# A padded buffer in a float32 two-layer decoder kernel: all later buffers move by 32 bytes in SBUF

## The chip, the cores and the metric

The kernel runs on one core of a Trainium2 chip. The metric is the device time of one execution in microseconds; lower is better. The kernel before takes 1462.85 us, the median of three runs (1462.66 to 1463.01).

## What is computed

Two decoder layers over 256 tokens of width 1024, in float32. The numerically large parts are plain matrix products; the rest is normalisation and two kinds of attention.

```python
for i in range(DEPTH):                                   # DEPTH = 2
    h = rms_norm(x, attn_norm[i])
    proj = h @ w_in[i]                                   # 1024 x 3072
    sb = rms_norm(stick_breaking_attention(...), sb_out_norm[i])
    df = rms_norm(differential_attention(...), diff_subln[i]) * (1 - lambda_init)
    x = x + concat(sb, df) @ w_out[i]                    # 1024 x 1024
    h2 = rms_norm(x, ffn_norm[i])
    if i % 2 == 0:
        x = x + (silu(h2 @ w_gate) * (h2 @ w_up)) @ w_down          # 1024 x 2816 x 1024
    else:
        x = x + moe_swiglu(h2, ...)                      # top 2 of 8 experts, 1024 x 3584 x 1024
return rms_norm(x, final_norm)
```

## The kernel before

**Weights.** All weights stream from HBM in pieces of 1 MB (128 partitions x 2048 float32). SyncE's queue loads piece n into one of the seven slots of `raw`; slot n % 7 is refilled once VectorE has finished with piece n - 7. TensorE runs these products on float32r data, and the kernel gets float32 accuracy by splitting: ScalarE writes `w_hi`, the rounded part of the piece (`split_hi`, L356), and VectorE writes `w_lo = raw - w_hi` (`split_lo`, L361), each into one of three slots. The activations are split in the same way (`aT_hi`/`aT_lo`, `hT_hi`/`hT_lo`, `xe_hi`/`xe_lo`, `he_hi`/`he_lo`). Each product is then three matmuls: high by high, low by high, high by low.

**Matmuls.** The helper `add` (L511) issues all of them. A matmul has a stationary operand of 128x128, loaded by its own LDWEIGHTS, and a moving operand that is streamed past it. Three callers matter:
- `rows_out` (the v projections, `w_out`, the dense feed-forward) and `expert_block` (the mixture of experts): the activation is stationary and the weights, `w_hi` or `w_lo`, move, 512 columns at a time (256 in the last dense piece).
- `columns_out` (the q and k projections): the weights are stationary and the activation, `aT_hi` or `aT_lo`, moves, 256 columns at a time.
- `scatter` (L927): at the very end, `onehotT` is stationary, and `ye_hi` or `ye_lo` moves, 512 columns at a time; eight matmuls in all, also on float32r data.

A row of the trace writes such a matmul as `ps<-w_hi,xe_hi`; the names do not tell which of the two moves. An expert block is 42 pieces of twelve 512-column matmuls each, interrupted by the transposes of the hidden rows (L950) after every sixth piece. Eight blocks run here.

**Where the buffers lie.** Buffers are allocated in the order of the code, one behind the other along the partition, and the allocator starts each at a multiple of 32 bytes. All offsets of slices that a matmul uses (multiples of 128 or 512 float32) are multiples of 512 bytes, so an operand's place within 64 bytes is that of its buffer. In the program as built, the first byte of the buffers that the text speaks of:

| Buffer | bytes from the partition's start | remainder by 64 |
|---|---|---|
| raw | 16512 | 0 |
| w_hi | 73856 | 0 |
| w_lo | 98432 | 0 |
| xs, hn | 123008, 131200 | 0, 0 |
| gC, the heads' norm weights (L132) | 143616 | 0 |
| cst (constants, among them the identity) | 143904 | 32 |
| aT_hi, aT_lo | 152096, 160288 | 32, 32 |
| xe_hi, xe_lo | 152096, 156192 | 32, 32 |
| hT_hi, hT_lo | 168480, 191008 | 32, 32 |
| ye_hi, ye_lo | 176672, 199200 | 32, 32 |
| yrow, xrow, ab, spl | 184864, 180768, 193056, 199200 | 32 |
| onehotT | 189984 | 32 |
| he_hi, he_lo | 191008, 195104 | 32, 32 |
| sil, hid | 203296, 207392 | 32, 32 |
| att | 211712 | 0 |

The buffer `gC` is written once (L1491, L1493) and read as a per-partition factor (L1024 and L1356 in the second half of each attention).

Of the kernel before, what the change touches and what calls it, by code (L numbers as in the profile page):

```python
# [27 lines left out]
P = 128  # L28
# [4 lines left out]
DEPTH = 2  # L33
# [80 lines left out]
def build(nc, x, w_in, w_out, attn_norm, ffn_norm, sb_out_norm, diff_subln, lambda_q1, lambda_k1,  # L114
          lambda_q2, lambda_k2, rel_bias, dense_w_gate, dense_w_up, dense_w_down, router_w,
          expert_w_gate, expert_w_up, expert_w_down, final_norm, consts, out):
    with ExitStack() as ctx:
        def sb(name, shape, dt=F32, stack=ctx):
            return stack.enter_context(nc.sbuf_tensor(name, shape, dt))
# [9 lines left out]
        hn = sb("hn", [P, TT, D])  # L129
        gain = sb("gain", [P, D])  # L130
        gT = sb("gT", [P, 2 * DEPTH, KT])
        gC = sb("gC", [P, 2, DEPTH])  # L132
        rw = sb("rw", [P, KT, NE])
        cst = sb("cst", [P, CONSTS])
        eps = sb("eps", [P, 1])
# [1707 lines left out]
```

## Time and profile before

| | |
|---|---|
| median of three runs | 1462.85 us |
| the profiled execution | 1462.97 us |
| its span, first to last instruction | 1460.8 us |
| around the span (1462.97 - 1460.8) | 2.2 us |
| TensorE busy | 1434.2 us, 98% of the span |
| VectorE, ScalarE busy | 1127.8 us, 934.4 us |
| 512-column and 256-column matmuls of L511 | 5160 and 864 |

The rows that are quoted further down come from one profiled execution. "PE" is TensorE's matmuls, "PEld" its weight loads, DVE VectorE, ACT ScalarE, POOL GpSimd, SPq SyncE's queue. Matmuls overlap, so the mean duration of one (about 395 ns) is longer than the distance between the starts of two in a row; the distance, called pitch below, is what a stream of matmuls costs.

### The profile page before, as it was taken

The numbers are of one execution on the slowest core, as the hardware profiler recorded it, in microseconds if no ns is written. First come the engines' busy times: TensorE is split into PE (matmuls) and PEld (weight loads), VectorE is DVE, ScalarE is ACT, GpSimd is POOL, SyncE is SP. The second block draws the span as 40 slices with busy tenths as digits, with TensorE's granted clock in tenths as the row PEclk, the third lists the DMA queues.
The fourth block names the chain that finished last, engine by engine and source line by source line (L and its number), as shares of the span: only waits on it lengthen the run. The fifth ranks groups of instructions, "written<-read, shape, count | busy, mean of one in ns | idle before, by whom it ended". The sixth has DMA issues, their size and how long they took to land.

```text
span 1460.8 us, 18431 instructions
## 1 busy us (share of the span) xinstructions
PE 1434.2 (98%) x6979; PEld 1179.6 (81%) x6979; DVE 1127.8 (77%) x852; ACT 934.4 (64%) x753; POOL 32.5 (2%) x51
## 2 busy tenths in 40 slices
PE   7999999999999999999999999999999999999996
PEld 7977888889888788888888888888888888888885
DVE  5664545536856899888888888888888888888896
ACT  4454544435554777777777777777777777767774
POOL 0010000000010020000000000000000000001000
PEclk9999999999999999999999999999999999999999
DMA  9642895555433899999999999999999999999992
GB/s 332 211 144 87 321 361 182 173 191 178 150 116 101 289 369 399 394 378 384 357 376 376 363 381 360 384 356 382 373 355 384 375 361 372 369 385 360 396 386 81
DMA packets 190909, 448.81 MB, mean 307 GB/s; under 512 B 8516, under 2 KB 11403, under 8 KB 190859
## 3 DMA queue, kind: packets, MB, share of 16 engines
q1 hardware_dynamic: 189034, 442.27, 83.4%
q0 software_dynamic: 1616, 5.77, 1.0%
q8 instruction: 34, 0.56, 0.2%
q10 hardware_dynamic: 208, 0.08, 0.0%
q14 instruction: 17, 0.13, 0.0%
HBM read 429.74 MB, written 18.36 MB: 307 GB/s over the span
## 4 chain that ended last, share of the span: by engine, by line
PE 95%; DMA 2%; DVE 2%; ACT 1%; SPq 1%; issue 0%; DVEq 0%
PE ps L511 88%; PE ps L950 2%; DMA raw<-in_w_in 1%; PE ps L634 1%; DMA hn<-bias_scratch 1%; PE ps L658 0%; PE ps L908 0%; PE ps L681 0%; PE ps L592 0%; PE ps L786 0%; DMA bias_scratch<-vrow 0%; DVE w_lo L361 0%; PE ps L623 0%; PE ps L645 0%; PE ps L876 0%; PE ps L646 0%
## 5 line engine op out<-in xcount | busy, mean ns | idle before, releaser
L361 DVE TENSOR_TENSOR w_lo<-raw,w_hi 128x2048 fp32r<-128x2048 f32 x401 | 916.0, 2291 | 233.8 <-ACT w_hi L356 232.2
L356 ACT ACTIVATE w_hi<-raw 128x2048 fp32r<-128x2048 f32 (+1 forms) x401 | 767.6, 1915 | 332.3 <-PE ps L511 327.6
L511 PE MATMUL ps<-w_hi,xe_hi 128*128 128x512 f32 x896 | 249.6, 400 | 0.3 <-DVE xe_lo L1744 0.3
L511 PE MATMUL ps<-w_hi,xe_lo 128*128 128x512 f32 x896 | 245.4, 395 | 0.0
L511 PE MATMUL ps<-w_lo,xe_hi 128*128 128x512 f32 x896 | 244.8, 394 | 0.0
L511 PEld LDWEIGHTS ps<-w_lo,xe_hi 128*128 128x128 f32 x896 | 168.2, 188 | 41.1
L511 PEld LDWEIGHTS ps<-w_hi,xe_lo 128*128 128x128 f32 x896 | 168.2, 188 | 40.5
L511 PEld LDWEIGHTS ps<-w_hi,xe_hi 128*128 128x128 f32 x896 | 164.6, 188 | 36.9 <-issue 0.5
L511 PE MATMUL ps<-w_hi,he_hi 128*128 128x512 f32 x448 | 123.5, 397 | 0.0
L511 PE MATMUL ps<-w_hi,he_lo 128*128 128x512 f32 x448 | 122.7, 395 | 0.0
L511 PE MATMUL ps<-w_lo,he_hi 128*128 128x512 f32 x448 | 122.4, 395 | 0.0
L511 PEld LDWEIGHTS ps<-w_lo,he_hi 128*128 128x128 f32 x448 | 84.1, 188 | 20.6
L511 PEld LDWEIGHTS ps<-w_hi,he_lo 128*128 128x128 f32 x448 | 84.1, 188 | 20.2
L511 PEld LDWEIGHTS ps<-w_hi,he_hi 128*128 128x128 f32 x448 | 83.5, 188 | 19.7
L511 PE MATMUL ps<-w_hi,aT_hi 128*128 128x512 f32 (+1 forms) x320 | 90.9, 393 | 4.6 <-DVE aT_lo L1356 4.0
L511 PE MATMUL ps<-w_hi,aT_lo 128*128 128x512 f32 (+1 forms) x320 | 88.6, 386 | 0.0
L511 PE MATMUL ps<-w_lo,aT_hi 128*128 128x512 f32 (+1 forms) x320 | 88.5, 386 | 0.0
L1024 ACT ACTIVATE he_hi<-ps 128x512 fp32r<-128x512 f32 x56 | 33.6, 600 | 69.5 <-PE ps L950 69.5
L511 PEld LDWEIGHTS ps<-w_hi,aT_hi 128*128 128x128 f32 x320 | 57.9, 188 | 17.4 <-DVE aT_lo L1356 4.5
L511 PEld LDWEIGHTS ps<-w_hi,aT_lo 128*128 128x128 f32 x320 | 60.7, 190 | 13.5
L511 PEld LDWEIGHTS ps<-w_lo,aT_hi 128*128 128x128 f32 x320 | 60.7, 190 | 13.2
L1265 ACT ACTIVATE sil<-ps 128x512 f32<-128x512 f32 x56 | 32.6, 582 | 14.0 <-PE ps L511 14.0
(237 smaller groups left out, 991.5 us busy)
## 6 DMA issues: line engine op xcount, KB each, us to landing
raw<-in_expert_w_gate SPq DMA_DIRECT2D x112, 1024.0 KB, 7.4
raw<-in_expert_w_up SPq DMA_DIRECT2D x112, 1024.0 KB, 7.5
raw<-in_expert_w_down SPq DMA_DIRECT2D x112, 1024.0 KB, 7.2
raw<-in_w_in SPq DMA_DIRECT2D x24, 1024.0 KB, 7.2
raw<-in_dense_w_gate SPq DMA_DIRECT2D x11, 1024.0 KB, 6.4
raw<-in_dense_w_up SPq DMA_DIRECT2D x11, 1024.0 KB, 8.0
raw<-in_dense_w_down SPq DMA_DIRECT2D x11, 1024.0 KB, 4.9
raw<-in_w_out SPq DMA_DIRECT2D x8, 1024.0 KB, 5.1
```

Of the source, the lines that this page charges most:

```text
L356: nc.scalar.activation(w_hi[:, n % SPL, 0:width], raw[:, n % RAW, 0:width], ACT.Copy).then_inc(hi_ready, 1)
L361: nc.vector.tensor_tensor(w_lo[:, n % SPL, :], raw[:, n % RAW, :], w_hi[:, n % SPL, :].bitcast(F32), ALU.subtract).then_inc(lo_ready, 1)
L511: return pe.matmul(o, stationary, moving, start=start, stop=stop, skip_group_check=True)
L634: pe.matmul(bank[:, 0:ZW], neg_tri, spl[:, g % 2, m, :], start=False, stop=False, skip_group_check=True)
L950: last = pe.transpose(ps[:, 7, f * P:f * P + P], hid[:, c % 2, f * P:f * P + P], ident)
L1024: return nc.scalar.activation(dst, src, ACT.Copy, scale=scale)
L1265: nc.scalar.activation(sil[:, c % 2, :], ps[:, c % 2, :], ACT.Silu).then_inc(esilu_done, 1)
```

## The change

`gC` had 4 float32 per partition (16 bytes, in a place of 32). It becomes the first four elements of a buffer `head_gains` of 16 float32 (64 bytes). No instruction is added, removed or moved on any engine, no DMA changes its size or its place in the queue, and every operand keeps its shape and type.

```diff
         gT = sb("gT", [P, 2 * DEPTH, KT])
-        gC = sb("gC", [P, 2, DEPTH])
+        head_gains = sb("head_gains", [P, P // 8])
+        gC = head_gains[:, 0:2 * DEPTH].rearrange("p (a l) -> p a l", a=2)
         rw = sb("rw", [P, KT, NE])
```

All buffers allocated behind `gC` move up by 32 bytes: `aT_hi`, `xe_hi`, `hT_hi`, `he_hi`, `ye_hi`, `onehotT`, `cst` and the others of the table with the remainder 32 now have 0, and `att`, for one, goes from 0 to 32, so that not quite all of them lie at multiples of 64. `raw`, `w_hi`, `w_lo`, `xs` and `hn` stay where they are.

## Rows read from the trace of the kernel before

**Rows 1.** The page: busy time by engine, and the granted clock in 40 slices.

```profile
PE 1434.2 (98%) x6979; PEld 1179.6 (81%) x6979; DVE 1127.8 (77%) x852; ACT 934.4 (64%) x753; POOL 32.5 (2%) x51
...
PEclk9999999999999999999999999999999999999999
```

**Rows 2.** The chain of work that ended last: share of the span by line.

```profile
by line: PE ps L511 88.3%; PE ps L950 1.7%; DMA raw<-in_w_in 0.8%; PE ps L634 0.7%; DMA hn<-bias_scratch 0.6%; PE ps L658 0.5%; PE ps L908 0.4%; PE ps L681 0.4%; PE ps L592 0.3%; PE ps L786 0.3%; DMA bias_scratch<-vrow 0.3%; DVE w_lo L361 0
```

**Rows 3.** The chain in order of time: start us, length us, what, matmuls.

```profile
150.36 30.80 PE ps L511 x132
...
631.58 16.80 PE ps L511 x72
648.81 16.80 PE ps L511 x72
```

**Rows 4.** Groups by shape: busy us, mean ns of one; matmuls, then weight loads.

```profile
L511 PE MATMUL ps<-w_hi,xe_lo 128*128 128x512 f32 x896 | 245.4, 395 | 0.0
...
L511 PE MATMUL ps<-aT_lo,w_hi 128*128 128x256 f32 x256 | 33.0, 281 | 0.0
...
L511 PE MATMUL ps<-w_hi,aT_lo 128*128 128x256 f32 x32 | 9.0, 281 | 0.0
...
L927 PE MATMUL ps<-ye_lo,onehotT 128*128 128x512 f32 x4 | 1.6, 390 | 0.0
...
L511 PEld LDWEIGHTS ps<-w_hi,xe_lo 128*128 128x128 f32 x896 | 168.2, 188 | 40.5
```

**Rows 5.** TensorE in order of time, the kernel's last matmuls: start us, us.

```profile
1444.11 1.10 PE L511 MATMUL ps<-w_hi,he_hi 128*128 128x512 f32 x4
...
1445.97 1.10 PE L511 MATMUL ps<-w_lo,he_hi 128*128 128x512 f32 x4
...
1450.01 0.39 PE L927 MATMUL ps<-ye_hi,onehotT 128*128 128x512 f32 x1
1450.24 0.39 PE L927 MATMUL ps<-ye_lo,onehotT 128*128 128x512 f32 x1
...
1451.15 0.39 PE L927 MATMUL ps<-ye_lo,onehotT 128*128 128x512 f32 x1
```

**Rows 6.** Windows: length, busy us (instructions) PE PEld DVE ACT POOL, clock, DMA share, GB/s.

```profile
1444.00:1447.00 3.00, 3.00 (x14) 2.13 (x12) 0.00 (x0) 0.00 (x0) 0.00 (x0) 1.00 0.00 0
...
520.00:620.00 100.00, 100.00 (x447) 80.86 (x446) 90.75 (x71) 72.84 (x50) 8.73 (x4) 1.00 1.04 392
...
600.00:1000.00 400.00, 400.00 (x1778) 323.30 (x1777) 346.54 (x191) 293.36 (x194) 0.00 (x0) 1.00 1.02 374
```

**Rows 7.** TensorE in order of time, two q and k projections.

```profile
48.56 2.08 PE L511 MATMUL ps<-aT_lo,w_hi 128*128 128x256 f32 x16
50.48 2.08 PE L511 MATMUL ps<-aT_hi,w_lo 128*128 128x256 f32 x16
...
69.16 2.04 PE L511 MATMUL ps<-aT_lo,w_hi 128*128 128x256 f32 x16
71.03 2.04 PE L511 MATMUL ps<-aT_hi,w_lo 128*128 128x256 f32 x16
```

**Rows 8.** Groups by shape, the same work at either remainder, ScalarE and GpSimd.

```profile
L1024 ACT ACTIVATE yrow<-ps 128x1024 f32<-128x1024 f32 x7 | 7.2, 1029 | 6.1 <-PE ps L511 6.1
...
L1156 ACT ACTIVATE hn<-ps 128x1024 f32<-128x1024 f32 x2 | 2.0, 1024 | 1.4 <-PE ps L681 1.4
...
L456 POOL TENSOR_SCALAR_AFFINE_SELECT att<-att 128x256 f32<-128x256 f32 x16 | 6.2, 409 | 32.2 <-ACT att L1105 32.2
L456 POOL TENSOR_SCALAR_AFFINE_SELECT spl<-spl 128x256 f32<-128x256 f32 x16 | 6.2, 408 | 321.1 <-DVE spl L1423 321.1
```

**Rows 9.** Waits, longest in total first: us, times, longest us.

```profile
ACT w_hi L356 <- PE ps L511: 327.6, 287, 8.1
...
ACT w_hi L356 <- DMA raw<-in_w_in: 4.5, 1, 4.5
...
SPq L380 <- DVE w_lo L361: 1139.5, 390, 15.5
```

## The prediction

> **What bounds the kernel now.** Read the page's first two parts first. TensorE is busy for 98% of the span, and the granted clock is at its upper level, 2.4 GHz, in all slices [rows 1]. Then the chain that ended last: 88.3% of it is one line, L511, the split matmuls [rows 2]. Whatever changes the time by more than a few microseconds must change what a matmul of L511 costs. The chain in order of time gives that cost: 72 matmuls in 16.80 us, 132 in 30.80, so 233.3 ns from one start to the next, in the dense and the expert feed-forward alike [rows 3]. That is longer than 512 columns at 2.4 GHz, which are 213.3 ns: each matmul loses 20 ns to something. Three candidates can be dropped by rows. It is not data: ScalarE waits 327.6 us for TensorE's freed slots, SyncE's queue waits 1139.5 us for VectorE to free slots, and ScalarE waits for a landing piece once, 4.5 us [rows 9]. It is not another engine or a DMA in the same memory: between 1444 and 1447 us VectorE, ScalarE, GpSimd and the DMA engines do nothing [rows 6], and the matmuls there start at 1444.11 and, eight later, at 1445.97, which is 1.86 us or 233 ns each, as everywhere [rows 5]. And the clock is 1.00 there. What is left is inside TensorE: the matmul, and the load of the next stationary operand that runs beside it.
>
> **What the change does.** It removes and adds no instruction. It moves `aT`, `hT`, `xe` and `he` from remainder 32 to remainder 0 by 64 bytes, while `w_hi` and `w_lo` stay at 0. Before, in every matmul of L511, one operand starts at remainder 0 and the other at 32: they are 32 apart. After it, both start at 0. This holds for either role, since `columns_out` only swaps which of them moves.
>
> **The other engines: nothing.** The trace has the same work at both remainders. ScalarE copies 1024 elements from PSUM into `yrow` (32) in 1029 ns and into `hn` (0) in 1024 ns, GpSimd masks `att` (0) in 409 ns and `spl` (32) in 408 [rows 8]. At most 5 ns in 1024, with another buffer's data, and both engines wait for TensorE anyway [rows 9]. VectorE's 401 splits touch only buffers that do not move. The buffers that DMAs fill with weights do not move either. I put all of this at 0, and at no more than 1 us either way.
>
> **The 512-column matmuls: the term that decides.** There is one place in the trace where both operands of such a matmul have the same remainder: L927, with `ye_hi` or `ye_lo` moving from 32 and `onehotT` stationary at 32. Its starts are 1450.01, 1450.24 and, five steps after the first of them, 1451.15 [rows 5]: 0.91 us for the last four steps, 227.5 ns each, or 1.14 for five, 228. Rounding of the starts alone makes these good to 2 or 3 ns. The durations say the same more sharply, since they are pitch plus a modelled tail: 390 ns for `ye_lo` against 395 for `xe_lo` [rows 4], 5 ns less on four matmuls of which the first is still settling after the stage's start. And the stage just ahead of it, just as undisturbed, runs at 233 [rows 5, 6]. So two operands with the same remainder appear to cost 6 ns less than two that are 32 bytes apart; I take a new pitch of 227.0, a gain of 6.3 ns. The rows bound it by 5 ns (durations) and 7 ns (starts and rounding) if the mechanism is real, and by 0 if it is not.
>
> The count: 3 x (896 + 448 + 288 + 88) = 5160 matmuls of 512 columns (one of the groups of 896 stands in [rows 4]). 5160 x 6.3 ns = 32.5 us. How much of it is on the path: all L511 matmuls cost 5160 x 0.2333 + 864 x 0.1185 = 1306.2 us, and the chain holds 88.3% of 1460.8 = 1289.9 us of them [rows 2], 98.8%. That leaves 32.1 us.
>
> **The 256-column matmuls.** 864 of them. Here the same addresses give several pitches: sixteen in 1.92 us (48.56 to 50.48), 120 ns each, and sixteen in 1.87 us (69.16 to 71.03), 117 ns [rows 7]. I take their middle, 118.5, for the mean. `columns_out` and the last dense piece, with the roles of the remainders swapped, have the same mean of 281 ns [rows 4], so it does not matter which of the two is at 32. Bounds: all could go to 120, + 864 x 1.5 = + 1.3 us, or gain as much as the wide ones, - 864 x 6.3 = - 5.4 us. I take - 2 us, nearer to the narrow spread that these rows show.
>
> **What comes next when TensorE is faster.** Six pieces and four transposes take 17.23 us now, from 631.58 to 648.81 [rows 3], and 17.23 - 72 x 0.0063 = 16.78 then. Between 600 and 1000 us VectorE is busy for 346.5 of 400 us and ScalarE for 293.4 [rows 6]; the same work in 16.78 / 17.23 = 0.974 of the time makes 89% and 75%. DMA moves 374 GB/s there and would have to move 374 / 0.974 = 384; one stretch of 100 us already shows 392 [rows 6]. The slack in [rows 9] covers it. If that cover were gone, DMA would be late next; the rival below prices that.
>
> **The sum.** 1462.97 - 32.1 - 2.0 = 1428.9 us, so 1429. Against the median of the runs the profiled execution is 0.1 us long, which is nothing here.
>
> **A rule that speaks against it.** The row shows 233.3 ns where 512 columns take 213.3 [rows 3]. The Trainium skill, "TensorE: Matmul & The Clock Gate", section "Step-by-step: what each phase is for", says that TensorE has two independent read ports, so that loading the next weights takes no bandwidth from the running matmul, and gives a warm pitch of about 216 ns. By that rule the two operands' relation in memory is nothing and the change gives 1463. The 233.3 ns in the same clock does not agree with its figure, so something that the rule leaves out is at work. "SBUF — State Buffer", section "Specifications (TRN2)", gives lines of 16 bytes; 32 is a multiple of that, and by lines alone no operand was badly placed before, which again would be 1463.
>
> **The rivals.** *Nothing happens: 1463.* The start of an operand within 64 bytes has no effect, and L927 is quicker for another reason: it loads the same stationary block four times in a row, and it is only eight matmuls long. Or only the moving operand's own start counts (32 in L927, 0 in the wide ones of L511, both before and after): then the wide ones keep 233.3, and only `columns_out` can move, 768 x 1.5 ns = + 1.2 us, 1464. For it: scalar and GpSimd work shows no effect of the remainder at all [rows 8]. Against it: no engine or DMA explains why L511 is slower than L927 in a quiet machine, and the equal means of both 256-column groups speak against a role of the moving operand alone.
>
> *DMA takes the place of TensorE: 1439.* The pitch falls, but the weights can't follow past 380 GB/s. The expert stage moves 374 GB/s [rows 6] for about 970 us (475 to 1447 us), so 374 x 970 / 380 = 955 us in place of 945 at 384: 10 us of the gain are gone. ScalarE would then wait for landings in that stage. Against it: 392 GB/s in [rows 6].
>
> *Slower: 1497.* The loss of 20 ns comes from the moving stream and the weight load meeting at the same place in memory, and starting both on the same 64-byte boundary is the worst case, not the best. The places are then told apart by more than 64 bytes: `xe_hi` after the change is 64 apart from `w_hi` by 128, `onehotT` is 0 apart from `ye_hi`, so L927 need not speak for it. One more loss of the size seen (6.7 ns, 233.3 to 240) in the 5160 matmuls is + 34 us. It decides if the pitch in the first expert block is above 233.3. Against it: L927 is the only sample with another distance, and it is quicker.
>
> **How the numbers follow.** Forecast, faster at 1429: 0.53. DMA-bound, 1439: 0.08. Nothing, 1463 to 1464: 0.28. Slower, 1497: 0.08, and 0.03 for smaller losses of the q and k projections that pass 0.2% (768 x 6.3 ns = 4.8 us). A measurement of this kernel can tell about 0.2% from no change, so 1460 to 1466 is the same. Faster 0.61, same 0.28, slower 0.11. If the mechanism is real the time lies between 1462.97 - 36.1 - 5.4 = 1421.5 (7 ns each, all of the narrow ones too) and 1439. The range must reach to the case of no change, since without it 4 in 10 would be left out: 1421 to 1464.
>
> **What would show it.** In the profile after, a stretch of 72 L511 matmuls on the chain should last 16.34 us and not 16.80, the group of `xe_lo` should show a mean near 389 ns and not 395 [rows 4], and its weight loads stay at 188 [rows 4]. The starts of the stretches should be 16.8 us apart and not 17.23. ScalarE's and VectorE's means should not move by more than a few ns. L927 should not change, since both its operands move together. The prediction is wrong if the pitch stays at 233.3 (the remainder is nothing), if it rises (the common start is the bad case), or if it falls and ScalarE waits for landings of expert weights (DMA).

## The result

The kernel after takes 1440.22 us (median of four runs, 1439.51 to 1440.69) against 1462.76 us before. The ratio is 0.9846, with a 95% interval of 0.9829 to 0.9863: 22.5 us or 1.5% faster. The forecast was 1429, a gain of 33.9 us: the direction came out, and two thirds of the size. How much of the mechanism did is told further down.

The page of the profiled execution after, which took 1440.63 us with a span of 1438.6: busy time by engine, the granted clock in 40 slices, and the chain of work that ended last. All lines of the code are one further down than before, so L512 here is L511 there.

```profile
PE 1411.4 (98%) x6979; PEld 1177.6 (82%) x6979; DVE 1126.6 (78%) x852; ACT 933.9 (65%) x753; POOL 34.7 (2%) x51
...
PEclk9999999999999999999999999999999999999998
...
PE ps L512 89%; PE ps L951 2%; DMA raw<-in_w_in 1%; PE ps L635 1%; PE ps L659 0%; DVE w_lo L362 0%; PE ps L909 0%; PE ps L682 0%; PE ps L593 0%; PE ps L787 0%; ACT w_hi L357 0%; PE ps L624 0%; PE ps L646 0%; PE ps L877 0%; PE ps L648 0%; PE ps L647 0%
```

The span is 22.2 us shorter, and TensorE's busy time, the first line against [rows 1], 22.8. VectorE and ScalarE are busy for about as long as before (1126.6 and 933.9 us against 1127.8 and 934.4). So the gain lies within TensorE's own work. The chain in order of time, to be set beside [rows 3]:

```profile
606.14 16.50 PE ps L512 x72
622.64 0.44 PE ps L951 x4
623.08 16.50 PE ps L512 x72
```

Seventy-two matmuls take 16.50 us in place of 16.80: 229.2 ns each in place of 233.3. The transposes between them still take 0.44 us. The groups by shape (busy us, mean ns of one) say the same, beside [rows 4]:

```profile
L512 PE MATMUL ps<-w_hi,xe_lo 128*128 128x512 f32 x896 | 240.7, 391 | 0.0
...
L512 PE MATMUL ps<-aT_lo,w_hi 128*128 128x256 f32 x256 | 32.3, 279 | 0.0
...
L512 PEld LDWEIGHTS ps<-w_hi,xe_lo 128*128 128x128 f32 x896 | 168.3, 188 | 37.1
```

These durations hold a modelled tail; the cost is in the starts. Worked out from the records of both traces, undisturbed 512-column matmuls of L511 start 233.4 ns apart on average before and 229.0 after, those of 256 columns 118.6 and 115.8. That is 5160 x 4.33 ns = 22.3 us and 864 x 2.8 ns = 2.4 us, 24.7 in all. When the first matmul of the last stage starts (L927, L928 after), the kernel after is 22.3 us ahead: 1427.11 against 1449.44. Of the other 2.4 us, 1.7 are hidden in the first stage: whatever TensorE saves there, it then waits for the bias row of VectorE, until 30.87 us after and 30.88 before. TensorE in order of time, first after, then before (start us, length us, idle time and what ended it):

```profile
30.87 1.22 PE L698 MATMUL ps<-diag,cst 128*128 128x256 f32 x2 [4.86 <-DVE vrow L1465]
```

```profile
30.88 0.99 PE L697 MATMUL ps<-diag,cst 128*128 128x256 f32 x2 [3.18 <-DVE vrow L1464]
```

About 0.5 us more go just behind this wait, where the granted clock is low for longer than before: these two matmuls and the sixteen behind them take 1.22 and 3.98 us against 0.99 and 3.72. 0.2 us stay unexplained. L928 itself then loses 0.6 us, and the work behind the last matmul is 0.5 us shorter, so that the spans differ by 22.2. The clock and L928 are told further down. A weight load lasts 188 ns in both.

### The profile page after: what moved, and what is told of

Read it like the earlier page. It is cut to its first block, busy times and chain, and to the rows that moved or that the text cites. A ratio compares the mean times of both kernels' runs of the same rounds, so it can differ in the third digit from the quotient of the medians.

```text
span 1438.6 us, 18431 instructions
## 1 busy us (share of the span) xinstructions
PE 1411.4 (98%) x6979; PEld 1177.6 (82%) x6979; DVE 1126.6 (78%) x852; ACT 933.9 (65%) x753; POOL 34.7 (2%) x51
## 4 chain that ended last, share of the span: by engine, by line
PE 95%; DVE 2%; ACT 1%; DMA 1%; SPq 1%; issue 0%; DVEq 0%; ACTq 0%
PE ps L512 89%; PE ps L951 2%; DMA raw<-in_w_in 1%; PE ps L635 1%; PE ps L659 0%; DVE w_lo L362 0%; PE ps L909 0%; PE ps L682 0%; PE ps L593 0%; PE ps L787 0%; ACT w_hi L357 0%; PE ps L624 0%; PE ps L646 0%; PE ps L877 0%; PE ps L648 0%; PE ps L647 0%
## 5 line engine op out<-in xcount | busy, mean ns | idle before, releaser
L512 PE MATMUL ps<-w_hi,xe_hi 128*128 128x512 f32 x896 | 247.0, 397 | 0.3 <-DVE xe_lo L1745 0.3
L512 PE MATMUL ps<-w_lo,xe_hi 128*128 128x512 f32 x896 | 241.8, 392 | 0.0
L512 PE MATMUL ps<-w_hi,xe_lo 128*128 128x512 f32 x896 | 240.7, 391 | 0.0
L512 PEld LDWEIGHTS ps<-w_lo,xe_hi 128*128 128x128 f32 x896 | 168.3, 188 | 37.4
L512 PEld LDWEIGHTS ps<-w_hi,xe_lo 128*128 128x128 f32 x896 | 168.3, 188 | 37.1
L512 PEld LDWEIGHTS ps<-w_hi,xe_hi 128*128 128x128 f32 x896 | 164.7, 188 | 33.3 <-issue 0.5
L512 PE MATMUL ps<-w_hi,he_hi 128*128 128x512 f32 x448 | 121.8, 394 | 0.0
L512 PE MATMUL ps<-w_lo,he_hi 128*128 128x512 f32 x448 | 120.8, 392 | 0.0
L512 PE MATMUL ps<-w_hi,he_lo 128*128 128x512 f32 x448 | 120.4, 391 | 0.0
L512 PEld LDWEIGHTS ps<-w_lo,he_hi 128*128 128x128 f32 x448 | 84.1, 188 | 18.7
L512 PEld LDWEIGHTS ps<-w_hi,he_lo 128*128 128x128 f32 x448 | 84.1, 188 | 18.5
L512 PEld LDWEIGHTS ps<-w_hi,he_hi 128*128 128x128 f32 x448 | 83.6, 188 | 17.5
L512 PE MATMUL ps<-w_hi,aT_hi 128*128 128x512 f32 (+1 forms) x320 | 90.4, 392 | 4.6 <-DVE aT_lo L1357 4.0
L512 PE MATMUL ps<-w_hi,aT_lo 128*128 128x512 f32 (+1 forms) x320 | 87.3, 383 | 0.0
L512 PE MATMUL ps<-w_lo,aT_hi 128*128 128x512 f32 (+1 forms) x320 | 86.9, 381 | 0.0
L512 PEld LDWEIGHTS ps<-w_hi,aT_hi 128*128 128x128 f32 x320 | 58.2, 189 | 16.7 <-DVE aT_lo L1357 4.5
L512 PEld LDWEIGHTS ps<-w_hi,aT_lo 128*128 128x128 f32 x320 | 60.7, 190 | 12.3
L512 PEld LDWEIGHTS ps<-w_lo,aT_hi 128*128 128x128 f32 x320 | 60.4, 189 | 12.0
```

The costliest lines, as they stand in the source:

```text
L512: return pe.matmul(o, stationary, moving, start=start, stop=stop, skip_group_check=True)
```

## The experiments

The theory after the result was that the distance between the two operands of a matmul sets its pitch, but over a longer stretch than 64 bytes. All slices of the matmuls step by 512 bytes, so I write the distance as (start of the stationary buffer - start of the moving one) by 512. In the decoder's 512-column matmuls it was 416 before and is 448 after. In L927, whose pitch the forecast borrowed, it is 0 in both. The rival theories: multiples of 64 as such help, or the moving operand's start alone, or something else among the moved buffers, or a weight load that is special in L927.

### A stream of matmuls at many distances

`m1_sweep` leaves the whole decoder out. It fills two buffers with float32r data and streams 72 matmuls for each pair of starts; between the segments stands one float32 matmul.

```
for m, s, w, kind in SEGMENTS:
    for i in range(72):
        at_m = m // 4 + (0 if kind == "one_moving" else (i % 4) * 512)
        at_s = s // 4 + (0 if kind == "one_stationary" else (i % 8) * 128)
        pe.matmul(ps[:, (i // 12) % 2, 0:w], stat[:, at_s:at_s + 128], moving[:, at_m:at_m + w], ...)
    mark()
```

> This kernel leaves the whole decoder out: it streams float32r matmuls whose operands lie in two buffers that start at multiples of 512 bytes, 72 matmuls for each pair of starting bytes (moving m, stationary s, columns w), with one float32 matmul between the segments. Steps are those of the decoder (moving 2048 bytes, stationary 512). Theory R (the loss comes from where the two streams lie relative to each other): s - m alone sets the pitch; m = 0, s = 416 (the relation of before) gives 233.3 ns, 448 (the relation of after) 229, 0 (the relation of L927) 227 or less, and m = 32, s = 128 or m = 16, s = 16 the same as m = 0 with the same difference. Theory M (each operand's own start within 64 bytes counts): all segments with m = 0 and s a multiple of 64 are equal, all with s = 32 by 64 equal. Theory N (what matters is that a stationary block is loaded again, as in L927): the segment with one stationary block is 227 at s = 32 as well, and the sweep over s is flat.

TensorE in order of time (start us, length us): the segments with the moving operand at 0 and the stationary one at 0, and at 416, 448 and 480, with their marks.

```profile
25.04 16.58 PE L98 MATMUL ps<-moving,stat 128*128 128x512 f32 x72
...
227.96 17.05 PE L98 MATMUL ps<-moving,stat 128*128 128x512 f32 x72
244.84 0.38 PE L90 MATMUL ps<-xt 128*128 128x128 f32 x2
244.98 16.73 PE L98 MATMUL ps<-moving,stat 128*128 128x512 f32 x72
261.55 0.38 PE L90 MATMUL ps<-xt 128*128 128x128 f32 x2
261.69 17.04 PE L98 MATMUL ps<-moving,stat 128*128 128x512 f32 x72
```

Nothing but the starting byte differs between these rows, and 72 matmuls take 16.58, 17.05, 16.73 or 17.04 us. The first of each run are still settling. The mean distance between the starts of the last 48, worked out from the records of the same trace (and of `m2_sweep`, below, for the gaps in the list), in ns:

```
512 columns, moving at 0; stationary at
   0: 226.7    32: 233.3    64: 233.3    96: 234.3   128: 232.4   160: 233.3   192: 228.9   224: 233.4
 256: 226.7   288: 233.4   320: 233.3   352: 234.3   384: 232.4   416: 233.3   448: 228.9   480: 233.3
   4: 232.3    16: 233.3    48: 233.3
other moving starts (moving, stationary)
 (32, 0) 233.3   (32, 32) 226.7   (32, 128) 234.4   (128, 32) 233.3   (128, 64) 228.9   (128, 128) 226.7
 (16, 0) 231.7   (16, 16) 233.3   (16, 48) 226.7
one block again and again: stationary (0, 0) 226.7, (0, 32) 233.3; moving (0, 32) 233.3
256 columns, moving at 0; stationary at
   0: 120.0    32: 118.3    64: 113.3    96: 117.4   128: 118.6   160: 120.0   192: 117.8   224: 116.7
 256: 120.0   288: 118.3   320: 117.8   352: 117.4   384: 118.7   416: 120.0   448: 117.8   480: 116.7
256 columns, other starts (moving, stationary)
 (32, 0) 117.8   (32, 32) 120.0   (0, 16) 118.3   (16, 16) 118.3
```

Three theories fall here. Multiples of 64 cost anything from 226.7 (0) to 233.3 (64). The repeated stationary block changes nothing. And the moving operand's own start does not decide: (32, 32) costs what (0, 0) costs. For 512 columns the stream reproduces the decoder's averages to 0.1 ns: 233.3 at 416, the distance of before, and 228.9 at 448, that of after. The theory that the distance alone counts holds for 512 columns at all six other pairs of starts at multiples of 32, and multiples of 32 are all that the allocator hands out. It does not hold at 16: (16, 16) is slow and (16, 48) quick. Any two distances that are 256 bytes apart cost the same to 0.1 ns, so for 512 columns these rows show a stretch of 256 bytes.

For 256 columns the distance alone is not enough. (32, 0) has the distance 480 and took 117.8 ns where (0, 480) took 116.7, and 64 and 320 differ (113.3 and 117.8). Each of these figures is a single run of 72, and the decoder, further down, has both 113 and 118 at one distance.

### The same distances in the decoder

`pad96`, `pad128` and `pad256` are the change with another size, so the later buffers move by 64, 96 and 224 bytes.

```diff
-        head_gains = sb("head_gains", [P, P // 8])
+        head_gains = sb("head_gains", [P, 24])      # pad96; 32 in pad128, 64 in pad256
```

> The heads' norm weights get 96 bytes: all later buffers lie 64 bytes further than before, at remainder 32 by 64 again. Theory R64 (relation by 64 bytes): 233.3 ns as before, 1463 us. Theory R128 or R512 (the relation counts over a longer stretch): another pitch than 233.3. Theory that any move helps: about 1440 us.

> The heads' norm weights get 128 bytes: the activations now lie a multiple of 512 bytes from the weights, as the two operands of L927 do before and after. Theory R64: 229 ns and 1440 us as after. Theory R128 or longer: 227 ns, the pitch of L927, and 1440 - 5160 x 2 ns = 1430 us, or less if L927 had not yet settled.

> The heads' norm weights get 256 bytes: later buffers lie at multiples of 64, as after the change, but the activations 128 bytes from the weights by 512. Theory that multiples of 64 are what helps: 1440 us. Theory R512, with the pitch that the stream of m1_sweep had at this relation (232.4 ns): 1440.2 + 5160 x (232.4 - 228.9) ns = 1458 us, give or take 3 us for the 256-column matmuls.

The chain in order of time, one stretch of 72 matmuls of each: `pad96`,

```profile
613.33 16.80 PE ps L512 x72
```

`pad128`,

```profile
607.53 16.37 PE ps L512 x72
```

and `pad256`.

```profile
612.93 16.73 PE ps L512 x72
```

Of these and the next two experiments only `pad128` was run more than once; seven runs of the kernel before beside them lay within 1.7 us. `pad96` (distance 480, remainder 32 by 64) ran in 1461.89 us beside 1462.15 of the kernel before: moving the buffers does nothing in itself. `pad128` (distance 0) took 1433.81 us, ratio 0.9804 (0.9788 to 0.9820): its matmuls settle at the 226.7 ns of the stream, and 72 take 16.37 us rather than 72 x 226.7 ns = 16.32 because a run needs up to ten steps to settle (one of these stretches has 235, 233, 236, 224, 231, 236, 228, 233 and 231 ns behind its first step, worked out from the records). The time is 3.8 us over the 1430 expected. The 256-column matmuls explain most of it: they are 119.8 ns apart here on average against 115.8 after, 864 x 4.0 ns = 3.5 us. The four runs of `pad128` lie in two pairs, at 1432.3 and 1432.4 and at 1435.2 and 1435.5, with a mean granted clock of 0.996 and 0.993; what made the clock differ stays open. `pad256` has all the activations at multiples of 64 and took 1458.62 us beside 1461.90. The forecast from the stream was 1458; the theory of multiples of 64 said 1440, and this refutes it in the decoder itself.

### Is it the relation, or the boundaries?

`both32` keeps the distance of after, 448, but starts both operands at remainder 32 by 64.

```diff
         raw = sb("raw", [P, RAW, PIECE])
+        skew = sb("skew", [P, 8])
         w_hi = sb("w_hi", [P, SPL, PIECE], F32R)
```

> As the change, with 32 more bytes between raw and w_hi: the weights' halves and all later buffers start at remainder 32 by 64, with the distances of after between them. Theory R (only the relation counts): 229 ns and 1440 us as after. Theory M (multiples of 64 are what helps): 233.3 ns or more and 1463 us or more.

The chain in order of time:

```profile
622.26 16.50 PE ps L513 x72
```

1439.72 us: as the change, with no operand of these matmuls on a multiple of 64. The distance counts, and the boundaries do not.

### Only the experts

`experts_only` is the kernel before with 32 bytes ahead of `xe_hi`.

```diff
+            gap_experts = se("gap_experts", [P, 8])
             xe_hi = se("xe_hi", [P, KT, P], F32R)
```

> The kernel before with 32 bytes ahead of xe_hi alone: only the expert stage's buffers move as the change moves them; aT, hT, cst and the rest stay. Theory R: 4032 of the 5160 matmuls go from 233.3 to 229.0 ns, 17.3 us, and the rest stays: 1444 to 1445 us. Theory that something else among the moved buffers (constants, attention, norms) gives the gain: near 1462 us.

The chain in order of time, in the expert stage:

```profile
611.85 16.50 PE ps L512 x72
```

1445.94 us beside 1462.04: 16.1 us of the 22.5 come from the expert matmuls. The expected 17.3 used 4.3 ns a matmul; 16.80 - 16.50 is 0.30 us for 72 or 4.2 ns, which makes 16.8. The other 6.4 us are near what the other matmuls give: 1128 x 4.33 ns = 4.9 and the 2.4 of the 256-column ones, less the 1.7 hidden in the first stage, 5.6 together. Within a microsecond nothing is left for constants, attention or norms.

### What part of the loss has to do with the weight load

> Again the decoder is left out; streams of 72 matmuls as in m1_sweep. Theory L (the weight load that runs beside the matmul takes the time, by reading near the place that the moving stream reads): with a stationary block of 64 or 32 columns the pitch at s = 416 falls from 233.3 towards 216, about half and a quarter of the 20 ns left, and the difference to s = 0 shrinks with it. Theory P (each float32r matmul costs this by itself): 233.3 and 226.7 for any number of stationary columns. bfloat16 operands, with half the bytes: by L at or near 216 ns for both starts. The 256-column sweep has no expectation but that s = 416 gives what the decoder's q and k projections do; it is to find their best place.

`m2_sweep` is the stream again with 64 or 32 stationary columns and with bfloat16 data. TensorE in order of time: 64 columns at 0 and 416, 32 columns at 0 and 416, and bfloat16 at 0 and 32, where one or two records are missing from the trace.

```profile
96.77 16.82 PE L105 MATMUL ps<-moving,stat 128*64 128x512 f32 x72
...
113.56 16.82 PE L105 MATMUL ps<-moving,stat 128*64 128x512 f32 x72
...
130.35 16.93 PE L105 MATMUL ps<-moving,stat 128*32 128x512 f32 x72
...
147.26 17.03 PE L105 MATMUL ps<-moving,stat 128*32 128x512 f32 x72
...
164.57 15.49 PE L105 MATMUL ps<-moving,stat 128*128 128x512 bf16 x70
...
180.11 15.70 PE L105 MATMUL ps<-moving,stat 128*128 128x512 bf16 x71
```

The theory that the load takes read time in proportion to its length is wrong. A quarter of the columns should have brought the pitch near 216 ns. It is 230.0 with 64 columns at either start, and 231.7 and 233.3 with 32: at distance 0 a shorter load is worse. The theory that each matmul costs this by itself, with 233.3 and 226.7 for any number of columns, is wrong too. In bfloat16 the steady matmuls are 216 ns apart at both starts tried, 0 and 32, a pair that is 6.6 ns apart in float32r. One expectation was set up wrongly: the q and k projections of before, where the weights are stationary, are at distance 96 (117.4 ns in the stream) and not at 416; only the last dense piece is at 416.

> The decoder is left out; streams as before. Theory F (a floor of 17/16 of the columns' time plus a wait of at most one step of 6.7 ns, which the relation sets): widths w at the best relation cost w x 17 / 16 / 2.4 ns, 141.7 at 320, 170.0 at 384, 198.3 at 448, and no relation costs more than 6.7 to 8 ns over that; with a stationary block of 64 or 32 columns another relation than 0 reaches 226.7, and none goes below. Theory L (the weight load takes the time): with 32 columns the best relation is well below 226.7, towards 216.

`m3_sweep` looks for a floor: other widths of the moving operand, and the short loads at more distances. In order of time: 320 columns at 0 and 64, 384 at 64, then 32 stationary columns at 32 and at 480.

```profile
79.16 10.80 PE L113 MATMUL ps<-moving,stat 128*128 128x320 f32 x72
...
89.94 10.80 PE L113 MATMUL ps<-moving,stat 128*128 128x320 f32 x72
...
124.23 12.73 PE L113 MATMUL ps<-moving,stat 128*128 128x384 f32 x72
...
345.27 17.45 PE L113 MATMUL ps<-moving,stat 128*32 128x512 f32 x72
...
480.85 16.57 PE L113 MATMUL ps<-moving,stat 128*32 128x512 f32 x72
```

The steady pitch is 146.7 ns at 320 columns and 173.3 at 384, the same at all three distances tried (0, 64, 448); at 448 columns it is 202.8, 202.2 and 200.0. Theory F had 141.7, 170.0 and 198.3 and is wrong in its factor; its bound of 8 ns over the floor fails as well, since 32 stationary columns reach 240.0. What fits is a fixed 13.3 ns over the columns' time at the best distance, for 320, 384, 448 and 512 columns alike (6.7 ns for 256). At 128 and 192 columns all six segments are at 111.7 ns and none of the three distances matters. With 32 stationary columns the pitch runs from 226.7 (distance 480) to 240.0 (distance 32), a wider spread than with 128. So no arrangement of 512 columns went below 226.7, and the length of the load moves the good distances about without removing the effect. That the stationary block's start and length matter says that its load takes part; how, is left open.

### A version that gains more

The tables disagree on the best distance. Wide matmuls want 0, where the 256-column ones, with the roles swapped, have their worst, 120.0; those want 64, which the change happens to give `aT` (448 seen from the wide side). `split` keeps the change for `aT` and puts `hT`, `xe` and `he` at distance 0.

```diff
+            gap_dense = sb("gap_dense", [P, 16], F32, phase)
             hT_hi = sb("hT_hi", [P, FT, S], F32R, phase)
...
+            gap_experts = se("gap_experts", [P, 16])
             xe_hi = se("xe_hi", [P, KT, P], F32R)
```

> The change with 64 more bytes ahead of hT_hi and ahead of xe_hi, so that the operands of the dense down projection and of the experts lie 0 from the weights by 512, and aT stays where the change put it. By the pitches of m1_sweep and pad128: 4296 matmuls at 226.7 and 864 at 228.9 ns, and the 768 of the q and k projections at 113.3 in place of pad128's 120: 1433.8 + 1.9 - 5.1 = 1430.6 us. Theory that only the 512-column term counts: 1435.7.

The projections, TensorE in order of time, first in `pad128`,

```profile
62.61 2.08 PE L512 MATMUL ps<-aT_lo,w_hi 128*128 128x256 f32 x16
64.53 2.08 PE L512 MATMUL ps<-aT_hi,w_lo 128*128 128x256 f32 x16
...
69.73 2.08 PE L512 MATMUL ps<-aT_lo,w_hi 128*128 128x256 f32 x16
```

then in `split`:

```profile
60.97 1.98 PE L514 MATMUL ps<-aT_lo,w_hi 128*128 128x256 f32 x16
62.78 1.98 PE L514 MATMUL ps<-aT_hi,w_lo 128*128 128x256 f32 x16
...
67.81 1.98 PE L514 MATMUL ps<-aT_lo,w_hi 128*128 128x256 f32 x16
```

From start to start sixteen take 1.92 us in `pad128`, 120 ns each, and 1.81 in `split`, 113. `split` took 1431.56 us (1430.99 to 1432.12), ratio 0.9794 (0.9778 to 0.9810), against the expected 1430.6. It beats both kernels by a clear margin; its interval does not touch that of the change (0.9829 to 0.9863), and its median is 8.7 us lower. Whether it beats `pad128` is not shown by the times: the medians differ by 2.2 us where 3.2 were expected, but the intervals of the ratios overlap, and `pad128`'s own runs differ by more than 3. What the traces do show is the pitch of the projections.

## Why the prediction was right, and where it was off

**What bounds the kernel: right.** Of 24.7 us that the matmuls of L511 lost, 22.3 had come through when the last stage began, or 90%. The prediction's factor for the path was 98.8%; the first stage, whose end another chain sets, took 1.7 us.

**The clock at its upper level throughout: a misreading, of little weight.** A digit 9 in the row PEclk of [rows 1] means 90% or more of full speed. Windows (columns as in [rows 6]) show short stretches at 1.2 GHz, first two of the kernel before, then two of the kernel after:

```profile
31.20:34.50 3.30, 3.30 (x16) 3.18 (x15) 2.56 (x2) 0.00 (x0) 0.50 (x1) 0.50 1.05 386
133.60:136.90 3.30, 3.30 (x9) 2.58 (x8) 2.29 (x1) 0.09 (x1) 0.00 (x0) 0.50 0.00 0
```

```profile
30.90:35.40 4.50, 4.50 (x19) 4.32 (x20) 3.13 (x6) 0.00 (x0) 0.56 (x1) 0.50 1.06 387
441.70:445.00 3.30, 3.30 (x9) 2.60 (x8) 2.29 (x1) 0.48 (x1) 0.00 (x0) 0.50 0.06 19
```

Eight 512-column matmuls there are 0.43 us apart, which costs 1.5 us. The kernel before pays this at 134 us and the kernel after at 442, so it cancels; a third stretch, at 468 and 462 us, is in both. Just ahead of 442 us TensorE had waited 2.00 us for `aT_lo`; the kernel before has the same wait at the same place (448.54) and the clock did not fall. The averages above leave these stretches out.

**The 20 ns as something inside TensorE that depends on where the operands lie: right in place, for a third of them.** Only the buffers' places changed, no other engine's time did, and `both32` and `pad96` separate the distance from everything else. But the best distance gives back 6.7 of the 20 ns; the other 13.3 stayed at every start tried. The rule of the Trainium skill that was weighed against the change ("TensorE: Matmul & The Clock Gate", section "Step-by-step: what each phase is for") would make the distance nothing. For float32r that does not hold: the stationary operand's starting byte alone moved the pitch between 226.7 and 234.3 ns. No trace shows the ports themselves. The rule's warm figure of about 216 ns was met by bfloat16.

**The new pitch of 227.0 ns: the step that was off.** It should have been 229.0, and this term, 5160 x 4.33 ns = 22.3 us, stood at 32.5. The mistake is in one inference: L927 and the kernel after agree by 64 bytes, and the forecast took that for the whole relation. By 512 they do not agree: L927 is at 0, the change gives 448. The forecast had noticed this (the slower rival says that `xe_hi` would be 64 apart from `w_hi` by 128) but used it only for the rival. With distance 0, `pad128` did reach 226.7, and its 1433.8 us is near the 1429 predicted. No row of before has two operands at 448, so its 229 could not be read there. What could have been done is a range for this term that admits a stretch longer than 64 bytes, with its most likely value between 233.3 and 227.

**Two pieces of luck.** First, the same remainder by 64 is not what helps. Of the eight distances that are multiples of 64, four save 4.4 ns or more (0, 192, 256, 448) and four save 0.9 or nothing; the change happened to land on one of the first four, `pad256` on one of the others. Second, L927 was a weak witness. Its distance is 0 in every kernel here, but eight matmuls need not settle. TensorE in order of time, L928 in `pad128`:

```profile
1422.42 0.40 PE L928 MATMUL ps<-ye_lo,onehotT 128*128 128x512 f32 x1
...
1423.82 0.40 PE L928 MATMUL ps<-ye_lo,onehotT 128*128 128x512 f32 x1
```

That is 1.40 us for six steps, 233 ns each, the pitch of L511 before. Had the kernel before shown this, nothing would have spoken for a gain. The rival that L927 is only eight matmuls long had a point about the sample, though not about the time.

**The range.** It held, but by its wide end: for a real mechanism the forecast gave 1421.5 to 1439, and 1440.2 lies just outside. That it is near the 1439 of the DMA-bound rival means nothing, since that rival's waits are absent, as shown below.

**The 256-column matmuls: - 2 us forecast, - 2.4 measured.** The size was right, partly by luck, and the reason only half. That it does not matter which operand is at 32 was read from equal mean durations; but the two roles are at different distances (96 and 416 before, 64 and 448 after), which the stream has at 117.4 and 120.0 ns, and at 113.3 and 117.8. TensorE in order of time after:

```profile
39.02 1.98 PE L512 MATMUL ps<-aT_hi,w_hi 128*128 128x256 f32 x16
40.83 1.98 PE L512 MATMUL ps<-aT_lo,w_hi 128*128 128x256 f32 x16
...
61.89 2.05 PE L512 MATMUL ps<-aT_lo,w_hi 128*128 128x256 f32 x16
63.77 2.05 PE L512 MATMUL ps<-aT_hi,w_lo 128*128 128x256 f32 x16
```

At one and the same distance some runs go at 113 ns (1.81 us for sixteen) and others at 118 (1.88), as [rows 7] had 117 and 120 before. In `split` those of the first layer settled at 113, and in the second layer some went at 118 again. What decides which of the rhythms a run falls into was not tried.

**The other engines, and DMA: right.** In the window from 600 to 1000 us (columns as in [rows 6]) DMA moved 381 GB/s, against 384 forecast for a larger gain:

```profile
600.00:1000.00 400.00, 400.00 (x1809) 328.98 (x1809) 352.24 (x195) 298.00 (x198) 0.00 (x0) 1.00 1.03 381
```

and ScalarE's only waits for landings are at the start, as in [rows 9]:

```profile
ACT w_hi L357 <- DMA raw<-in_w_in: 5.7, 2, 5.5
```

The DMA-bound rival is excluded. So is the slower one as priced: its mechanism, that more than 64 bytes count, was real, but the distance drawn was a good one. At 32 stationary columns a distance exists that costs 240 ns, the figure of that rival; with the 128 columns of the decoder the worst found is 234.3.

**L927 unchanged: only in part.** Its first matmuls after are 0.23 us apart as before, then the granted clock falls from 2.4 to 1.2 GHz. Windows ahead of the stage and in it (columns as above), and the matmuls across the fall:

```profile
1424.00:1427.00 3.00, 0.73 (x4) 0.26 (x2) 1.18 (x1) 1.02 (x1) 0.00 (x0) 1.00 0.00 0
1427.00:1428.00 1.00, 0.90 (x4) 0.77 (x5) 0.05 (x1) 0.00 (x0) 0.00 (x0) 1.00 0.00 0
1428.00:1430.00 2.00, 2.00 (x6) 1.07 (x4) 1.28 (x1) 0.17 (x1) 0.00 (x0) 0.51 0.00 0
```

```profile
1427.44 0.39 PE L928 MATMUL ps<-ye_lo,onehotT 128*128 128x512 f32 x1
1427.67 0.39 PE L928 MATMUL ps<-ye_hi,onehotT 128*128 128x512 f32 x1
...
1428.60 0.63 PE L928 MATMUL ps<-ye_lo,onehotT 128*128 128x512 f32 x1
1429.03 0.63 PE L928 MATMUL ps<-ye_hi,onehotT 128*128 128x512 f32 x1
```

TensorE had waited for `ye_lo` before it, with 0.73 us of work in three. The kernel before has the same wait of 2.37 us, and there the clock stayed up until the last matmul was over. The eight matmuls' starts span 2.34 us here against 1.71. These 0.6 us come from the clock and not from the operands' distance, which is the same.

## What to carry to other kernels

Where a stream of float32r matmuls runs at more than the columns' time, measure the pitch at several distances between the stationary and the moving buffer before anything else is tuned: a few bytes of padding were worth 1.5 to 2.1% here, and a stream without the rest of the kernel gave the decoder's figure for 512 columns within 0.7 ns each time, though not for 256. Look at the distance over at least 512 bytes and for each width and role by itself, since the best one for 512 columns was the worst for 256. A single quick sample elsewhere in a kernel shows that a better pitch exists; it gives its size only if it agrees in everything that may count and is long enough to settle, which took up to ten steps here.

## What the runs showed of the hardware

- The pitch of back-to-back float32r matmuls of 512 columns depends on the distance between the operands in SBUF: 226.7 ns at 0 and 256 bytes, 228.9 at 192 and 448, 232.4 to 234.3 at all other multiples of 32, with the same clock and nothing else running. For 256 columns it is 113.3 ns at 64 in the stream (113 or 118 in the decoder) and 116.7 to 120.0 elsewhere, and there the distance alone does not fix it; at 320 and 384 columns none of the three distances tried made a difference.
- At the best distance a wide matmul costs 13.3 ns more than its columns at 2.4 GHz (146.7, 173.3, 200.0 and 226.7 ns for 320, 384, 448 and 512). Bfloat16 matmuls of 512 columns are 216 ns apart at both starts tried.
- Settled float32r runs of 512 columns with a 128-column stationary block repeat a pattern of one to twelve matmuls whose sum is a multiple of 6.67 ns, and at 256 columns the same distance can settle into more than one pattern. What beats in this rhythm remains open.
- The granted clock fell behind one wait of TensorE and not behind a wait of the same length at the same place in the other kernel (2.00 us at 441 and 449 us; 2.37 us ahead of L927).
- A shorter weight load (32 columns in place of 128) does not make the matmul beside it quicker, and moved the pitch up to 240.0 ns at one distance.
